# Two attentions behind a feed-forward block: a head is turned two steps behind its scores, the other products are spread over all steps, and a sigmoid moves behind the exponentials

## The reference, cut to what matters

```python
proj = h @ w_in[layer]                       # 256 x 4000
q_a, k_a, v_a, c_q, c_kv, k_pe, gate_a, gate_b = jnp.split(proj, splits, axis=-1)
y_a = moba_attention(q_a, k_a, v_a)          # 8 heads of 64; causal softmax at 256 tokens
y_b = mla_attention(c_q, c_kv, k_pe, ...)    # 8 heads of 96 (64 + 32 rotary), causal softmax
merged = (jax.nn.sigmoid(gate_a) * (y_a @ w_branch_a[layer])
          + jax.nn.sigmoid(gate_b) * (y_b @ w_branch_b[layer]))
x = x + merged @ w_out[layer]
```

## Time and profile before

| | us |
|---|---|
| median of 3 runs | 1438.17 (1435.8 to 1440.6) |
| the profiled execution's own time | 1438.28 |
| its span in the trace | 1436.6 |
| PE busy | 1382.3 (96%) |
| DVE busy | 978.4 (68%) |
| ACT busy | 638.3 (44%) |
| POOL busy | 153.0 (11%) |

### The profile page before, as it was taken

How to read it: one execution, slowest core, us unless ns; L and a number is a source line. 1 busy time by engine, 2 the same in 40 slices (tenths; PEclk the granted TensorE clock), 3 DMA queues, 4 the chain that set the end, 5 groups by cost and what they waited for, 6 DMA issues and landing times.

```text
span 1436.6 us, 22740 instructions
## 1 busy us (share of the span) xinstructions
PE 1382.3 (96%) x9510; PEld 967.8 (67%) x9510; DVE 978.4 (68%) x1555; ACT 638.3 (44%) x851; POOL 153.0 (11%) x138
## 2 busy tenths in 40 slices
PE   6999899999999999869999999999999999999998
PEld 5656798688864455535988889999997444444443
DVE  2433686389985756557489988899997555555555
ACT  2342422176654433454336454444444444444443
POOL 0221432114530000000010300000000000000000
PEclk9999998899999999979999999999999999999999
DMA  6322000375666431324526655555456555675551
GB/s 259 131 79 88 1 1 1 131 262 193 210 232 212 158 125 60 116 90 163 188 99 242 210 192 198 170 172 174 164 180 229 203 203 199 201 246 200 202 203 56
DMA packets 33141, 231.51 MB, mean 161 GB/s; under 512 B 3712, under 2 KB 3984, under 8 KB 6160
## 3 DMA queue, kind: packets, MB, share of 16 engines
q1 hardware_dynamic: 31968, 227.02, 45.5%
q10 hardware_dynamic: 720, 1.73, 0.3%
q0 software_dynamic: 352, 1.32, 0.2%
HBM read 227.96 MB, written 2.10 MB: 160 GB/s over the span
## 4 chain that ended last, share of the span: by engine, by line
PE 90%; DVE 4%; ACT 3%; issue 2%; DMA 0%; POOL 0%; ACTq 0%; DVEq 0%; POOLq 0%
PE bank L584 22%; PE bank L587 22%; PE bank L590 22%; PE bank L607 5%; PE bank L684 2%; PE bank L1225 2%; PE bank L912 2%; PE bank L1014 2%; PE bank L743 2%; PE bank L1189 1%; PE bank L883 1%; PE bank L701 1%; PE bank L809 1%; PE bank L800 1%; PE bank L1178 1%
## 5 line engine op out<-in xcount | busy, mean ns | idle before, releaser
L584 PE MATMUL bank<-arena 128*128 128x256 f16 (+3 forms) x632 | 186.4, 303 | 1.9 <-DVE arena L1333 1.6
L590 PE MATMUL bank<-arena 128*128 128x256 f16 (+3 forms) x632 | 186.4, 302 | 0.0
L587 PE MATMUL bank<-arena 128*128 128x256 f16 (+3 forms) x632 | 186.4, 302 | 0.0
L1333 DVE SCALAR_TENSOR_TENSOR arena<-ring,arena 128x2048 f16<-128x2048 f32 (+1 forms) x59 | 133.8, 2273 | 37.0 <-ACT arena L2253 36.9
L2253 ACT ACTIVATE arena<-ring 128x2048 f16<-128x2048 f32 (+1 forms) x59 | 111.3, 1891 | 30.5 <-PE bank L590 30.5
L2073 DVE SCALAR_TENSOR_TENSOR HT<-ring,HT 128x2048 f16<-128x2048 f32 x41 | 93.9, 2290 | 40.9 <-ACT HT L2617 40.8
L2646 ACT CAST arena<-arena 128x512 f16<-128x512 f32 x64 | 39.4, 618 | 170.9 <-PE bank L590 170.9
L2073 DVE SCALAR_TENSOR_TENSOR ring<-ring 128x2048 f16<-128x2048 f32 x42 | 96.1, 2289 | 27.7 <-ACT ring L2617 27.4
L2073 DVE SCALAR_TENSOR_TENSOR X<-ring,X 128x2048 f16<-128x2048 f32 x42 | 96.1, 2289 | 26.1 <-ACT X L2617 26.0
L1225 PE MATMUL bank<-ring,arena 128*128 128x128 f16 x512 | 98.6, 219 | 0.0
L584 PE MATMUL bank<-cst,X 128*128 128x256 f16 x336 | 91.5, 272 | 0.0
(11 more groups left out here) (351 smaller groups left out, 3318.9 us busy)
## 6 DMA issues: line engine op xcount, KB each, us to landing
ring<-in_expert_u SPq DMA_DIRECT2D x64, 1024.0 KB, 4.9
ring<-in_expert_v SPq DMA_DIRECT2D x64, 1024.0 KB, 4.9
ring<-in_w_in_n SPq DMA_DIRECT2D x24, 1024.0 KB, 4.9
ring<-in_w_up_t SPq DMA_DIRECT2D x22, 1024.0 KB, 4.9
ring<-in_w_down_n SPq DMA_DIRECT2D x11, 1024.0 KB, 5.0
ring<-in_w_out_n SPq DMA_DIRECT2D x8, 1024.0 KB, 4.9
ring<-in_w_query_t SPq DMA_DIRECT2D x8, 1024.0 KB, 5.2
ring<-in_w_in_t SPq DMA_DIRECT2D x3, 1024.0 KB, 7.0
```

Of the source, the lines that this page charges most:

```text
L584: pe.matmul(out_, stat[0], mov[0], start=start, stop=False)
L587: pe.matmul(out_, stat[0], mov[1], start=False, stop=False)
L590: return pe.matmul(out_, stat[1], mov[0], start=False, stop=stop)
L1333: nv.scalar_tensor_tensor(out=lo, in0=ld.slot(i), scalar=W_UP, in1=hi, op0=ALU.mult, op1=ALU.subtract).then_inc(s["split_lo"], 1)
```

## The change: what it does

- A head's transposes come two steps behind its scores in both attentions (`lag=2`), and its weighted sum three steps behind. The loop therefore has 16 steps and not 15.
- The 19 filler steps in the loop are dealt out anew: no step is without one. PE does them behind the attention's part of a step, as before (`filler_first=False`); DVE and ACT now do theirs ahead of the attention's part.
- Of the `branch_a` products two are inside the loop and two behind `y_T` of mla (before: two inside the loop, one ahead of that `y_T`, one behind it). On DVE their gating moves behind the loop.
- The copying away of a filler product's bank (`evicted`) moves to the next filler step.
- On ACT the sigmoid comes one filler step later, which is behind the last exponential. Also, the eviction `second(3)` comes ahead of the four of `moba_T`.

```diff
-FILLING = [2, 1, 2, 1, 2, 2, 1, 2, 1, 2, 1, 0, 1, 0, 1]
+FILLING = [1, 1, 2, 2, 1, 1, 1, 1, 1, 1, 1, 2, 1, 1, 1, 1]
-def second_mixers(moba, latent, filler):
+def second_mixers(moba, latent, filler, filler_first=True):
     for n in FILLING:
-        next(moba, None)
-        next(latent, None)
+        if not filler_first:
+            next(moba, None)
+            next(latent, None)
         for _ in range(n):
             next(filler)
+        if filler_first:
+            next(moba, None)
+            next(latent, None)
...
-        for step in range(n_heads + 2):
-            if step >= 2:
-                weighted(step - 2)
-            if 1 <= step <= n_heads:
-                turned(step - 1)
+        for step in range(n_heads + lag + 1):
+            if step > lag:
+                weighted(step - lag - 1)
+            if lag <= step < n_heads + lag:
+                turned(step - lag)
             if step < n_heads:
                 scores(step)
             yield
...
     fill = filler()
-    second_mixers(moba(), latent(), fill)
-    next(fill)
+    second_mixers(moba(), latent(), fill, False)
     y_T("mla", m.YB)
     run(fill)
...
@@ vector_program, filler
         for g in range(4):
             for half in range(2):
+                if g and not half:
+                    evicted(g - 1)
                 if g or half:
                     split_lo(42 + 2 * g + half)
                 yield
-                if half:
-                    use = ("proj2b", g, 1)
-                    evict(use, m.P2[:, 1, at:at + w], ps.tile(*use)[:, 0:w], UN)
                 yield
+        evicted(3)
         split_lo(50)
+        yield
         for t in range(2):
             lo_T(("moba", "y_T", t), m.yh, m.yl, 0, t)
         split_lo(51)
         yield
-        for g in range(2):
-            for t in range(2):
-                if (g, t) == (0, 0):
-                    split_lo(52)
-                gated("branch_a", g, t)
-                yield
+        split_lo(52)
+        yield
...
@@ scalar_program, filler
+        evicted(3)
         split_hi(50, ps.full("proj2b", 3, 1))
+        yield
         for t in range(2):
             hi_T(("moba", "y_T", t), m.yh, 0, t)
         split_hi(51)
+        split_hi(52)
+        yield
         for t in range(2):
             for g in range(4):
                 na.wait_ge(*ps.free("proj2b", g, t))
             na.activation(m.gates[:, t, :], m.gates[:, t, :], ACT.Sigmoid).then_inc(s["gates"], 1)
         yield
-        split_hi(52)
-        for _ in range(4):
-            yield
...
+    second(3)
     moba_T()
-    second(3)
```

More of the change, by code:

```diff
@@ L691, in whole_T, with attention @@
                 turn((name, t, c0), [src[:, t, (c0 + i) * 128:(c0 + i + 1) * 128] for i in range(n)])
-    def attention(p, n_heads, rows, vN, bias, base):
+    def attention(p, n_heads, rows, vN, bias, base, lag=1):
         qT, kT = m.qT[p], m.kT[p]
@@ L1072, in moba @@
             pe.wait_ge(*ps.free("proj2", 3, t))
-        yield from attention("moba", 8, 64, lambda h, t: m.P2[:, t, 1440 + h * 64:1440 + (h + 1) * 64], None, 4)
+        yield from attention("moba", 8, 64, lambda h, t: m.P2[:, t, 1440 + h * 64:1440 + (h + 1) * 64], None, 4, 2)
     def latent():
@@ L1109, in latent @@
                 pe.wait_ge(*ps.free("mla_T", n, i))
-        yield from attention("mla", 8, 96, lambda h, t: m.KV[:, t, h * 128 + 64:(h + 1) * 128], None, 0)
+        yield from attention("mla", 8, 96, lambda h, t: m.KV[:, t, h * 128 + 64:(h + 1) * 128], None, 0, 2)
     def y_T(p, y):
@@ L1372, in log_sigmoid, with attention @@
         return nv.scalar_tensor_tensor(out=dst, in0=x, scalar=0.0, in1=dst, op0=ALU.min, op1=ALU.subtract)
-    def attention(p, n_heads, scale, base):
+    def attention(p, n_heads, scale, base, lag=1):
         sums, mx, rec, sc = m.sums[p], m.mx[p], m.rec[p], m.sc[p]
@@ L1411, in weighted @@
                     .broadcast_to([128, 2, 4, 64]), ALU.mult).then_inc(ps.empty(*use), 1)
[L1413 to L1417, removed]
+        for st in range(n_heads + lag + 1):
+            if st > lag:
+                weighted(st - lag - 1)
+            if lag <= st < n_heads + lag:
+                turned(st - lag)
             if st < n_heads:
@@ L1877, in latent @@
         yield
-        yield from attention("mla", 8, 1.0 / math.sqrt(96.0), 0)
+        yield from attention("mla", 8, 1.0 / math.sqrt(96.0), 0, 2)
     def gated(name, g, t):
@@ L1892, in filler, with evicted @@
     def filler():
+        def evicted(g):
+            at, w = SECOND_AT[g + 4], SECOND_GROUPS[g + 4]
+            use = ("proj2b", g, 1)
+            evict(use, m.P2[:, 1, at:at + w], ps.tile(*use)[:, 0:w], UN)
         for g in range(4):
-            at, w = SECOND_AT[g + 4], SECOND_GROUPS[g + 4]
             for half in range(2):
+                if g and not half:
+                    evicted(g - 1)
                 if g or half:
@@ L1938, in vector_program @@
     fill = filler()
-    second_mixers(attention("moba", 8, 0.125, 4), latent(), fill)
-    next(fill)
+    second_mixers(attention("moba", 8, 0.125, 4, 2), latent(), fill)
     for t in range(2):
         lo_T(("mla", "y_T", t), m.yh, m.yl, 4, t)
-    run(fill)
+    for g in range(2):
+        for t in range(2):
+            gated("branch_a", g, t)
     split_lo(53)
@@ L2259, in soft, with attention @@
         na.activation(ap, ap, ACT.Ln, bias=1.0).then_inc(s["soft_ln"], 1)
-    def attention(p, n_heads, base):
+    def attention(p, n_heads, base, lag=1):
         sums, mx, sc = m.sums[p], m.mx[p], m.sc[p]
@@ L2276, in turned @@
                 evict((p, "turned", h), m.pt[p][h % 3], ps.tile(p, "turned", h)[:, 0:384])
-        for st in range(n_heads + 2):
-            if 1 <= st <= n_heads:
-                turned(st - 1)
+        for st in range(n_heads + lag + 1):
+            if lag <= st < n_heads + lag:
+                turned(st - lag)
             if st < n_heads:
@@ L2534, in latent @@
         yield
-        yield from attention("mla", 8, 0)
+        yield from attention("mla", 8, 0, 2)
     def hi_T(use, hi, c0, t):
@@ L2542, in filler, with evicted @@
     def filler():
+        def evicted(g):
+            at, w = SECOND_AT[g + 4], SECOND_GROUPS[g + 4]
+            use = ("proj2b", g, 0)
+            evict(use, m.P2[:, 0, at:at + w], ps.tile(*use)[:, 0:w], UN)
         for g in range(4):
-            at, w = SECOND_AT[g + 4], SECOND_GROUPS[g + 4]
             for half in range(2):
@@ L2551, in filler @@
                 yield
-                if half:
-                    use = ("proj2b", g, 0)
-                    evict(use, m.P2[:, 0, at:at + w], ps.tile(*use)[:, 0:w], UN)
+        evicted(3)
         split_hi(50, ps.full("proj2b", 3, 1))
+        yield
         for t in range(2):
@@ L2576, in scalar_program @@
     split_hi(42, ps.full("proj2", 1, 1))
+    second(3)
     moba_T()
-    second(3)
     fill = filler()
-    second_mixers(attention("moba", 8, 4), latent(), fill)
-    next(fill)
+    second_mixers(attention("moba", 8, 4, 2), latent(), fill)
     for t in range(2):
         hi_T(("mla", "y_T", t), m.yh, 4, t)
-    run(fill)
     split_hi(53, ps.full("branch_a", 0, 1))
```

## The result

The changed kernel takes 1423.76 us (median of 11 runs, 1421.54 to 1431.65), the kernel before 1437.82 us (11 runs, 1435.8 to 1443.43): ratio 0.9913, 95% interval 0.9892 to 0.9934. The forecast was 1423.9. The profiled execution of after is not the median one: 1429.71 us, with a span of 1428.1.

The account below looks back on a forecast made before the run. PE was taken to bound the kernel, with 24.9 us idle and 8.2 lost to the clock between 505 and 650. Saving 11.1 idle plus 4.8 clock less 1.5 handovers, 14.4, takes 1438.28 to 1423.9 us; range 1415 to 1434.

Parts of the forecast that it names:

- (a): `second(3)` ahead of `moba_T` on ACT: PE's wait for that bank goes, gain 1.2 us; the 1.0 behind it remains.
- (b): `lat_kv`'s wait for ACT goes, as a filler product now lies between it and `lat_q`: gain 1.2 us.
- (c): `mla_T`'s wait for DVE's rotation and POOL's copies stays, 3.4 us, plus 0.9 for the last three transposes: loss 1.2.
- (d): Steps 8 to 11, two attentions: a 3.5 us wait goes, three tiles emptied late cost 2.7 together: gain 0.8 us.
- (e): The end, last mla heads: waits of 3.5, 2.1 and 0.2 us leave 5.8 of 14.9; gain 9.1, sigmoid costing nothing.
- (f): PE's granted clock: the dip of (c) and one behind (e) stay, 3.4 of 8.2 us left; gain 4.8.
- (g): Around ten handovers between engines on the path, assumed 0.15 us each: 1.5 us taken off the gain.
- R1: Rival: the leads hold better, most waits of (d) and (e) vanish, 8 us more saved: 1416 us; chance 0.13.
- R2: Rival: lead spent in part, split work delays heads' maxima, four more 1.5 us waits and a dip: 1431.6 us; chance 0.20.
- R4: Rival: slower, DVE's scores and tiles stand behind a split awaiting PE's product, 4.7 us each: 1446 us; chance 0.06.
- R3: Rival: nothing gained, the waits only move: 1434 to 1442 us; chance 0.11.

Follow-up runs that it names:

- after_again: The changed kernel, unaltered, run and traced a second time: 1422.90 us, ratio 0.9894 to the kernel before; stretch 134.9 us.
- scores_first: Changed kernel, but in the fifth step DVE does the attention's part ahead of its `split_lo`: 1421.32 us, ratio 0.9869 to the kernel before.
- sigmoid_only: Kernel before with only ACT's sigmoid moved one filler step later, behind the last exponentials: 1442.08 us, ratio 1.0023.
- lag_sigmoid: Kernel before with the two-step lead in both attentions and the sigmoid one filler step later, old deal of products: 1432.28 us, ratio 0.9970.
- lag_only: Kernel before with only the second step of lead in both attentions: 1430.99 us, ratio 0.9927; stretch 136.0 us.
- tiles_first: Changed kernel with `split_hi(50)` and `split_lo(50)` one filler step later, behind the halves of `y_T`: 1427.91 us, ratio 0.9933 to the kernel before.
- spread_only: Changed kernel with the lead taken back to one step (15 steps, the last with two products): 1435.63 us, ratio 0.9958 to the kernel before.
- three_moves: Changed kernel with DVE's rotation a step earlier, the fiftieth splits one filler step later, and fifth-step scores ahead of `split_lo`: 1414.75 us, ratio 0.9841 to kernel before.

## Why the prediction was right

The time (1423.9 against 1423.76) and the gain (14.4 against 14.5 us in the stretch) are nearer than the steps are, since errors of both signs cancelled. That closeness is luck, and partly the luck of the execution: the second trace's gain is 11.0. The mechanism, which holes stay and what ends them, is what the prediction had right in the main. Step by step, from the first trace:

- (a) Right: no wait at `moba_T`, and the 1.0 behind it stayed (0.98).
- (b) Half right: the wait of `lat_kv` for ACT went (1.2), but a new one came at `lat_q` (L1093), 0.70 us here and up to 2.6 in other executions. The new deal has one filler product fewer ahead of `lat_q`, and the DMA of the weights, which POOL starts once `proj2` is done, is still under way: `lat_q` started 8.0 us behind the start of the second of these DMAs before (523.38 and 515.36), and 5.9 behind it after (525.84 and 519.96), and the DMA takes 5.6 us there and 7.5 in after_again. The step looked at `lat_kv` and at ACT alone.
- (c) Mis-sized, 3.4 + 0.9 forecast and 5.50 measured. 3.38 is what is left when POOL's copy is not held up (scores_first), so the reckoning of DVE was right and the 2.1 us are POOL's. I named the copies and took them for unchanged. The 0.9 us did not show in after.
- (d) Too careful: 2.7 forecast, 0.96 measured, one of the three late tiles.
- (e) Right in place and cause, 5.8 forecast, 2.89 + 1.99 = 4.9 measured. "The sigmoid itself then costs nothing" holds for after and was wrong as a statement on the edit: alone it loses 3.9 us in the stretch. By the traces of sigmoid_only and lag_sigmoid its cover is that `split_hi(52)` and both last tiles come ahead of it, on which the step was silent. No run moves the gating by itself.
- (f) Too high, 4.8 forecast, 2.7 measured. One dip behind (e) was right, but it lasted 5 us at half the clock and not 4 at 0.57, and the one behind (c) cost 2.3 us and not 1.7. That isn't the length of the hole: behind 3.4 us the dip cost 2.9 in scores_first and 1.5 in lag_only.
- (g) No run shows the 0.15 us for a handover, and nothing was seen of the 1.5 us: idle time and clock alone explain 14.6 of 14.5. Handovers that can be read off the lines above take 0.05 (ACT's tile ends at 615.80, PE starts at 615.85) and 0.10 us (618.95 and 619.05), and they are part of the holes already.

Idle time left was 13.0, forecast 13.8. R1 (leads hold better) was nearest among the others: (d) shows some of it. R2 and R4 wanted several waits for L1297 in the middle of the stretch, and there is one of 0.96. R4's mechanism, DVE behind a split ahead of an odd tile, is real all the same: sigmoid_only pays 7.4 us for it and tiles_first 3.2. R3 is excluded by the interval.

Whether the parts need each other is shown for the sigmoid's place alone. In the stretch the lead alone gives 9.9 us and all the rest without the lead 0.0, and together they give 14.5 or 11.0, so that 1 to 5 us would come only from having both; but one kernel's stretch varies by 3.5. By the times the lead takes 0.73% and the rest 0.42%, and both together 0.87% or 1.06% in two sets of runs: they add up within their intervals. What the traces do show is the sigmoid's place: alone or with the lead it loses, since a `split_hi` and a tile stand behind it, and in the new deal the later place is worth 3.0 us of idle time. That a longer lead makes PE tolerant of late work, and that the deal puts the work where this tolerance is, fits these numbers and is argued. What remains open is why some executions of unchanged code lose more clock in the first block than others, why holes of the same length cost the clock so differently, and how long the weights' DMA takes.

## What to carry to other kernels

When work is reordered on one engine, ask for each moved instruction which other engine's work now runs at the same time, POOL's copies above all: an unmoved copy took 2.1 us more because a two-input DVE operation moved next to it, and a stalled PE paid it in full. A moved instruction pushes back all that stands behind it on its engine: the sigmoid pushed back a `split_hi` and a tile, and a `split_lo` moved off one tile ended up ahead of another. Follow what stands and waits behind the new place, in program order, on each engine. Measure the stretch that the change touches between two fixed instructions, trace the same kernel a second time before reading anything from differences of a few us, and hold the stretch of one trace against the times of all runs: spread_only looks like no gain in the one and like 0.4% in the other.

## What the runs showed of the hardware that I had not expected

- POOL's copy of 128x512 f32 within SBUF took 0.61 to 0.63 us, and 2.74 when a `scalar_tensor_tensor` with both inputs in SBUF had started 0.03 us before on DVE. It was the same in five traces.
- The first block, the same code in all kernels, lost 7.7, 11.1, 14.5 or 18.0 us to the clock between 140 and 300 us (give or take 0.2), and the rest of the program started up to 8.6 us later for it.
- Less idle time in more pieces can be worth nothing: the trace of spread_only has 5.2 us less than the kernel before and loses 4.3 more to the clock. The opposite holds in three_moves, where holes up to 3.2 us left the clock at 1.00.
